# A hybrid encoder step on one core: the later attention's loads, scale rows and gate values in another order

## The chip, the cores and the metric

The kernel runs as one program on one core of a Trainium2 chip. Its time is the device time of one execution in microseconds (us); lower is better. The kernel before took 3911.17 us (median of 3 runs, 3910.19 to 3914.08).

## The reference

One layer of a streaming encoder over two request groups that share the weights: 512 prompt rows and 8 x 16 sample rows, that is 640 rows of 2048 in f32. In the kernel they are five tiles of 128 rows (four prompt tiles, one sample tile).

```
sh1, sc1, g1, sh2, sc2, g2 = split(silu(c) @ w_ada + b_ada)
h = rmsnorm(x, norm1_g) * (1 + sc1) + sh1
za, zg, q, k, v = split(h @ w_in)                   # 2048 -> 5 x 1024
y_conv = silu(layernorm(causal_dwconv(za * sigmoid(zg))))
o = band_attention(q, k, v, bias, 16 heads of 64)
x = x + g1 * (concat(y_conv, o) @ w_out)            # 2048 -> 2048
h2 = rmsnorm(x, norm2_g) * (1 + sc2) + sh2
x = x + g2 * peer(h2)
y = rmsnorm(x, final_g)
```

`peer` makes key queries h2 @ w_pq (2048 -> 2048), scores them against 2 x 128 keys for each of 8 heads, and takes the best 16 of the sums, so each row has 8 x 16 = 128 picks among 16384 experts. For each pick the row of `u_experts` (2048 values) is multiplied with h2 and summed (a dot), gelu of it times the softmax weight is the pick's weight, and the weighted rows of `v_experts` are summed.

## The kernel before

**Two halves.** Tiles 0 and 1 are the first half, tiles 2, 3 and 4 the later half (`TX = 2`, `TY = 3`). The first half goes ahead through attention, output projection, second norm, key queries and key scores. While TensorE (PE) then works on the later half, VectorE (DVE) picks and works off the dots of the first half.

**Dots.** There are 640 steps (`step(n)`, line 2180): 40 groups of 16, one group for each tile and head. A step waits for one gather, in which each of 128 partitions gets one row of `u_experts` (128 x 2048 f32, 1.05 MB), multiplies and sums it (line 2201), and does a piece of the choosing for a coming group. GpSimd (POOL) issues the gathers (line 776) into four buffers: gather n waits for dot n - 4. Steps are laid by hand between DVE's other work, by `steps(k)` calls. Dots 0 to 255 belong to the first half; step 266 begins the build of the first weight matrix.

**The later half on PE.** Query, key and value projection (`quarter_columns`, `quarter_rows`, lines 1119 and 1126), then 16 attention heads, then the output projection: four blocks of 512 columns, each loaded in four quarters of 1 MB, times three tiles, so 12 results (v = 0 to 11 on DVE). DVE adds each to the residual (lines 2292 and 2293) and lays `steps(4)` behind each of the first nine. PE may be six results ahead of it (`o_free`). Behind v = 10 and v = 11 and the last comes `norm_tile` (line 1922), the second norm of tiles 2, 3 and 4. PE turns the tiles over and multiplies them with `w_pq` in four blocks (line 1119); ScalarE (ACT) copies queries and scores out (`keep_queries`, line 1498).

**The entry to attention.** PE makes the first scores of head 0, runs `stay_busy(5, 22)` (22 products of the identity into bank 5, which nothing reads), and then the part of head 0's scores with the cached keys, whose end releases DVE. DVE comes from its 124th dot, clears a buffer, packs the sample queries (line 2265), waits for head 0's bias (line 2241), and reduces the maximum (lines 2252 to 2256). In each head it lays two more dots.

**SyncE's queue (SP).** SP issues nearly all loads of the later half in written order, each behind its own waits: the w_in quarters; the first three value stores (`values_out(0)`); the first w_out block (`load_block(6, ...)`); three more value stores; for each head its bias, and for each pair of heads cached keys and values; behind attention the rows x and g1 (5 MB), then the w_out blocks 7, 8 and 9 with the scale rows (`A2Y`, `n2Y`) and shift rows (`B2Y`) of the second norm between them, then the first block of `w_pq`. Head h's bias waits until the maximum of head h - 2 is done. A quarter waits until PE has used the quarter that it overwrites.

**Behind it.** PE builds a matrix W of pick weights for two tiles (`build`, 64 rounds of one-hot products with DVE and ACT) and multiplies it with all of `v_experts`, 128 pieces of 1 MB (`dense`, line 1328); this twice, for tiles 0 and 1 and for 2 and 3. Tile 4 is done with 128 gathers of `v_experts` rows on DVE (line 2321). `gate_exp(1)` and `gelu(1)` (lines 1590 and 1594) are tile 1's exp of the softmax and gelu of the dots; the latter waits for 256 dots. Step 266 needs both.

Of the kernel before, what the change touches and what calls it, by code (L numbers as in the profile page):

```python
# [5 lines left out]
def hybrid_encoder_step(nc, ins, outs):  # L6
# [56 lines left out]
    with ctx:  # L63
# [312 lines left out]
        def _(sp):  # L376
# [131 lines left out]
            values_out(0)  # L508
            load_block(6, "w_out", 0)
            values_out(1)  # L510
# [16 lines left out]
            for h in range(NH):  # L527
                hp, b = divmod(h, 2)
                if h >= 2:
                    sp.wait_ge(mx_ready, NH + h - 1)  # L530
                sp.dma_start(biasP[:, b], rows(ext_d, [[EXT - 1, P]], 512, h * P * EXT + 127)).then_inc(s_b[b], 16)
                sp.dma_start(biasC[:, b], biasC_d[h]).then_inc(s_b[b], 16)
                if b == 0 and h + 2 < NH:
                    k_cache(hp + 1)
                if b == 1:
                    values(hp)

            def spread(dst, i, s):
# [9 lines left out]
            for b in range(7, 10):  # L548
                load_block(b, "w_out", (b - 6) * PW)
                if b == 7:  # L550
                    spread(A2Y, 1, s_sc2)
                    sp.dma_start(n2Y, n2rows_d[:, :]).then_inc(s_n2, 16)
                if b == 8:
                    sp.wait_ge(s_A2, 3)
                    sp.dma_start(B2Y[0], modrows_d[2, 0]).then_inc(s_sh2, 16)
# [254 lines left out]
        def _(pe):  # L810
# [359 lines left out]
            def scores(h):  # L1170
                hp, b = divmod(h, 2)
                r = slice(DH * b, DH * b + DH)
                q, k = catY[r, CT + hp], kT[r, hp]
                pe.wait_ge(mx_ready, NH + h)
                pe.matmul(PB[0][:, 0:512], q[:, 128:256], k[:, 0:512], start=True, stop=True)
                pe.matmul(PB[1][:, 0:384], q[:, 0:128], k[:, 0:384], start=True, stop=True)
                pe.matmul(PB[2][:, 384:512], q[:, 256:384], k[:, NP:NT], start=True, stop=True)
                if h == 0:
                    stay_busy(5, 22)
                pe.wait_ge(s_qx, hp + 1)  # L1180
                pe.wait_ge(kct_E, hp + 1)
                for s in range(NB):
                    m = pe.matmul(PB[2][:, 256:384], qX[r, s], kCT[r, hp % 2, s], start=(s == 0), stop=(s == NB - 1))  # L1183
                m.then_inc(sc_ready, 1)
# [157 lines left out]
        def _(act):  # L1342
# [155 lines left out]
            def keep_queries(G, dst, tiles):  # L1498
                for n in range(16):
                    act.wait_ge(q_done, 16 * G + n + 1)  # L1500
                    if n >= 2:
# [143 lines left out]

            gate_exp(1)
            gelu(1)
            copy_turned(0)
# [43 lines left out]
        def _(dve):  # L1692
# [539 lines left out]
            for g in range(2):  # L2232
                for k in range(18):
                    choose(g, k)
            steps(124)

# [38 lines left out]
            for h in range(NH):  # L2275
# [6 lines left out]
                steps(1)  # L2282
            steps(16)

# [3 lines left out]
            for v in range(4 * TY):  # L2288
# [4 lines left out]
                TT(x[:, at], x[:, at], wtmp[:, v % 2], ALU.add).then_inc(o_free, 1)  # L2293
                if v == 4:
                    dve.wait_ge(s_sc2, 16 * 2)
                    dve.wait_ge(s_n2, 16)
                    for b in range(2):
                        STT(out=A2Y[b], in0=A2Y[b], scalar=1.0, in1=n2Y, op0=ALU.add, op1=ALU.mult).then_inc(s_A2, 1)
                if v < 3 * TY:
                    steps(4)  # L2300
                elif v == 3 * TY:
                    steps(2)
                    dve.wait_ge(s_A2, 3)
                    dve.wait_ge(s_sh2, 16)
                elif v < 4 * TY:
                    norm_tile(TX + v - 3 * TY - 1, A2Y[0], B2Y[0])
                    steps(1)
            dve.wait_ge(s_sh2, 16 * 2)
# [47 lines left out]
```

## Time and profile before

| What | Value |
|---|---|
| median of 3 runs | 3911.17 us |
| the profiled execution's own time | 3912.98 us |
| its span (first to last instruction) | 3911.2 us |
| PE busy | 3659.4 us, 94% |
| DVE busy | 2665.0 us, 68% |
| ACT / POOL busy | 444.2 / 1022.0 us |
| mean DMA rate, bytes moved | 363 GB/s, 1418.49 MB |
| issuing queues | POOL's gathers q0 848.17 MB; SP's q1 563.29 MB |

All times in the rows are us from the span's start. The span lies 1.8 us under the execution's own time. A row of a timeline has the start, the duration, engine, line and operation, out<-in, and in brackets how long the engine had been idle and what ended that. "SPq" rows are the issuing of transfers, not the transfers. The busy shares are means over the whole span; the change touches some 600 us of it, from 1210 to 1850 us.

### The profile page before, as it was taken

The page shows a single profiled execution, that of the slowest core. Times are in us where ns is not written, and L with a number is a line of the kernel's source. Part 1 is how long each engine was busy: PE and PEld are TensorE (multiplying, and loading weights), DVE is VectorE, ACT ScalarE, POOL GpSimd, SP SyncE. Part 2 cuts the span into 40 slices and gives each one's busy share as a digit, 9 for nine tenths or more (in the row PEclk, how much of TensorE's full clock was granted, in tenths as well). Part 3 has the DMA queues.
Part 4 walks back from the last instruction along what each step waited for, and adds up shares of the span by engine and source line. Part 5 has one row for each costly group of instructions (what it writes and reads, how often), then busy time and mean ns, then how long its engine had stood idle before and what let it go on. Part 6 is the DMA issues. An engine that isn't in the chain of part 4 may idle for free.

```text
span 3911.2 us, 34419 instructions
## 1 busy us (share of the span) xinstructions
PE 3659.4 (94%) x12521; PEld 1929.5 (49%) x12521; DVE 2665.0 (68%) x4253; ACT 444.2 (11%) x975; POOL 1022.0 (26%) x888
## 2 busy tenths in 40 slices
PE   5899999998998898899989999999998899999996
PEld 2566545476543663466734444444465344444443
DVE  1258853157888788878986777767688754555666
ACT  2100004110000440102600000000052000000000
POOL 1000001215324344343232222222233322222331
PEclk8999999998999799999999999999999999999998
DMA  9878773559999899999799999999989999999997
GB/s 387 274 247 275 256 290 128 198 204 405 413 414 417 331 379 413 395 406 361 266 415 421 414 411 422 421 419 418 417 294 358 421 421 380 421 422 422 421 417 310
DMA packets 337760, 1418.49 MB, mean 363 GB/s; under 512 B 26009, under 2 KB 134529, under 8 KB 195742
## 3 DMA queue, kind: packets, MB, share of 16 engines
q0 software_dynamic: 120752, 848.17, 53.8%
q1 hardware_dynamic: 215840, 563.29, 37.8%
q10 hardware_dynamic: 1008, 4.98, 0.3%
q8 instruction: 91, 1.49, 0.2%
q14 instruction: 69, 0.57, 0.0%
HBM read 1390.84 MB, written 47.28 MB: 368 GB/s over the span
## 4 chain that ended last, share of the span: by engine, by line
DMA 50%; PE 31%; issue 12%; DVE 5%; POOL 2%; ACT 1%; DVEq 0%; POOLq 0%; SPq 0%; ACTq 0%
DMA R<-in_u_experts,MS 36%; DMA R<-in_v_experts,MS 10%; PE bank L895 8%; PE bank L926 7%; PE bank L1119 4%; PE bank L1298 3%; DMA R<-in_w_ada 2%; DVE R L2321 2%; PE bank L840 1%; POOL R L776 1%; DVE R L2201 1%; PE bank L1294 1%; PE bank L812 1%; PE bank L1183 1%; DMA R<-in_w_in 1%
## 5 line engine op out<-in xcount | busy, mean ns | idle before, releaser
L776 POOL DMA_INDIRECT R<-in_u_experts,MS x640 | 817.9, 1278 | 1699.1 <-DVE MS L2201 1477.7
L2201 DVE CUSTOM_DVE_ANT_0 R<-R 128x2048 f32<-128x2048 f32 x374 | 856.6, 2291 | 383.3 <-DMA R<-in_u_experts,MS 361.8
L1328 PE MATMUL bank<-R,RB 128*128 128x512 f32 x2304 | 1024.6, 603 | 48.2 <-DMA R<-in_v_experts 48.2
L1328 PE MATMUL bank<-RB 128*128 128x512 f32 x1792 | 778.2, 592 | 0.0
L1328 PEld LDWEIGHTS bank<-R,RB 128*128 128x128 f32 x2304 | 443.1, 193 | 619.6 <-issue 559.1
L2201 DVE CUSTOM_DVE_ANT_0 R<-R,RB 128x2048 f32<-128x2048 f32 x266 | 608.6, 2288 | 124.2 <-DMA R<-in_u_experts,MS 123.4
L1328 PEld LDWEIGHTS bank<-RB 128*128 128x128 f32 x1792 | 340.5, 190 | 428.6 <-issue 428.6
L2321 DVE SCALAR_TENSOR_TENSOR R<-R,MS 128x2048 f32<-128x2048 f32 x128 | 301.5, 2355 | 198.1 <-DMA R<-in_v_experts,MS 197.7
L895 PE MATMUL bank<-RB,R 128*128 128x256 f32 (+1 forms) x1536 | 399.8, 421 | 23.2 <-DMA R<-in_w_pq 18.8
L895 PEld LDWEIGHTS bank<-RB,R 128*128 128x128 f32 x1536 | 294.0, 193 | 122.6 <-DMA R<-in_w_pq 19.3
L1119 PE MATMUL bank<-RB,R 128*128 128x384 f32 x1024 | 334.9, 487 | 10.1 <-DMA R<-in_w_in 8.8
L1126 PE MATMUL bank<-R,RB 128*128 128x512 f32 x576 | 255.7, 606 | 23.5 <-DMA R<-in_w_out 13.9
L926 PE MATMUL bank<-R,RB 128*128 128x512 f32 x640 | 275.8, 592 | 0.5 <-issue 0.5
L1119 PEld LDWEIGHTS bank<-RB,R 128*128 128x128 f32 x1024 | 192.7, 190 | 144.5 <-DMA R<-in_w_in 13.4
L776 POOL DMA_INDIRECT R<-in_v_experts,MS x128 | 135.1, 1056 | 384.2 <-DVE R L2321 359.3
L926 PEld LDWEIGHTS bank<-R,RB 128*128 128x128 f32 x640 | 121.1, 190 | 151.4 <-issue 151.4
L1126 PEld LDWEIGHTS bank<-R,RB 128*128 128x128 f32 x576 | 111.2, 194 | 166.6 <-issue 137.2
L1829 DVE SCALAR_TENSOR_TENSOR RB<-RB,MS 128x512 f32<-128x512 f32 x240 | 175.8, 732 | 0.0
L1298 PE MATMUL bank<-R 128*128 128x128 f32 x1024 | 137.0, 277 | 2.2 <-DVE R L2084 2.2
L1753 DVE TENSOR_TENSOR RB<-bank,RB 9x256 f32<-9x256 f32 x128 | 53.5, 418 | 112.1 <-PE bank L840 108.0
L1298 PEld LDWEIGHTS bank<-R 128*128 128x128 f32 x1024 | 125.9, 194 | 2.8 <-DVE R L2084 2.8
L812 PE MATMUL bank<-MS,RB 128*128 128x128 f32 (+5 forms) x493 | 71.6, 291 | 34.8 <-DMA RB<-in_rel_bias_table 17.5
(355 smaller groups left out, 2248.5 us busy)
## 6 DMA issues: line engine op xcount, KB each, us to landing
R<-in_v_experts SPq DMA_DIRECT2D x144, 1024.0 KB, 9.1
RB<-in_v_experts SPq DMA_DIRECT2D x112, 1024.0 KB, 9.1
R<-in_w_ada SPq DMA_DIRECT2D x48, 2048.0 KB, 14.0
R<-in_w_in SPq DMA_DIRECT2D x20, 2048.0 KB, 18.8
R<-in_w_in SPq DMA_DIRECT2D x24, 1024.0 KB, 33.4
R<-in_w_out SPq DMA_DIRECT2D x8, 2048.0 KB, 8.4
R<-in_w_pq SPq DMA_DIRECT2D x8, 2048.0 KB, 10.6
R<-in_w_out SPq DMA_DIRECT2D x16, 1024.0 KB, 33.0
```

Of the source, the lines that this page charges most:

```text
L776: pool.indirect_dma_start(dst, None, table, bass.IndirectOffsetOnAxis(ap=expert[T_ % 2][:, c:c + 1], axis=0)).then_inc(signal, 16)
L812: return pe.transpose(out, in_, ident[0:k, 0:k])
L895: m = pe.matmul(PB[2 * par + i][:, 0:src.shape[-1]], w, src[:, k], start=(k == 0), stop=(k == KT - 1))
L926: m = pe.matmul(PB[bank][:, :], src[:, 8 * half + i, t * P:(t + 1) * P], wide[:, slot, i, :], start=(half + i == 0), stop=(half + i == 8))
L1119: m = pe.matmul(PB[bank][:, 0:NY], quad[:, q, i, c * P:(c + 1) * P], src[:, 4 * q + i], start=(q + i == 0), stop=(q + i == 6))
L1126: m = pe.matmul(PB[bank][:, :], src[:, 4 * q + i, t * P:(t + 1) * P], quad[:, q, i, :], start=(q + i == 0), stop=(q + i == 6))
L1298: x = pe.matmul(PB[m % 2][:, k * P:(k + 1) * P], oneh[m % 3][:, 1, k], oneh[m % 3][:, 0, k], start=True, stop=True)
L1328: x = pe.matmul(PB[4 * h + q][:, :], W[:, i, h * P:(h + 1) * P], vring[slot][:, q * PW:(q + 1) * PW], start=(i == 0), stop=(i == NKEY - 1))
L1753: t = TT(m, PB[4 + b][32 * g:32 * g + NCND, 0:BW], m, ALU.add)
L1829: ch.mark(STT(out=oP, in0=iP, scalar=w, in1=oP, op0=ALU.mult, op1=ALU.add))
L2201: V.tensor_tensor_reduce(u, u, x, 1.0, 0.0, ALU.mult, ALU.add, dots[t % 2][:, h * TOPK + s:h * TOPK + s + 1]).then_inc(dots_done, 1)
L2321: STT(out=acc, in0=pick_rows[p % NPICK], scalar=weight[TP][:, p:p + 1], in1=acc, op0=ALU.mult, op1=ALU.add).then_inc(v_used, 1)
```

## The change

SP: block 6 of w_out is loaded behind head 3's loads and no longer ahead of the last value stores; the scale rows come behind block 8 and not behind block 7; the first shift rows behind block 9 and not block 8. DVE: 116 dots ahead of attention (124 before), 28 behind it (16), two fewer at v = 9 and one fewer each behind v = 10 and v = 11; the A2 product stands behind v = 7 and not v = 4. Both orders have 212 dots when the last norm tile begins. PE: 34 filler products in head 0 (22), and 2 more ahead of head 1. ACT: tile 1's exp and gelu before the 13th key query of the later half and not behind all 16.

```diff
@@ SP
             values_out(0)
-            load_block(6, "w_out", 0)
             values_out(1)
...
                 if b == 1:
                     values(hp)
+                if h == 3:
+                    load_block(6, "w_out", 0)
...
             for b in range(7, 10):
                 load_block(b, "w_out", (b - 6) * PW)
-                if b == 7:
+                if b == 8:
                     spread(A2Y, 1, s_sc2)
                     sp.dma_start(n2Y, n2rows_d[:, :]).then_inc(s_n2, 16)
-                if b == 8:
+                if b == 9:
                     sp.wait_ge(s_A2, 3)
                     sp.dma_start(B2Y[0], modrows_d[2, 0]).then_inc(s_sh2, 16)
@@ PE, scores(h)
+                if h == 1:
+                    stay_busy(5, 2)
                 pe.wait_ge(mx_ready, NH + h)
...
                 if h == 0:
-                    stay_busy(5, 22)
+                    stay_busy(5, 34)
@@ ACT, keep_queries
                 for n in range(16):
+                    if G and n == 12:
+                        gate_exp(1)
+                        gelu(1)
...
-            gate_exp(1)
-            gelu(1)
             copy_turned(0)
@@ DVE
-            steps(124)
+            steps(116)
...
-            steps(16)
+            steps(28)
...
-                if v == 4:
+                if v == 7:
                     dve.wait_ge(s_sc2, 16 * 2)
...
                 elif v == 3 * TY:
-                    steps(2)
                     dve.wait_ge(s_A2, 3)
                     dve.wait_ge(s_sh2, 16)
                 elif v < 4 * TY:
                     norm_tile(TX + v - 3 * TY - 1, A2Y[0], B2Y[0])
-                    steps(1)
```

SP's queue at the entry to attention, before. `out_new_v` are the value stores, `ext_scratch` and `biasC_scratch` a head's bias, `k_cache` and `v_cache` the cached rows of a pair.

```order
57 L485 DMA R<-in_w_out 128x4x512 x4
58 L496 DMA out_new_v_prompt<-RB 128x512 x2
59 L496 DMA out_new_v_sample<-RB 128x512
60 L531 DMA RB<-ext_scratch 128x512
61 L532 DMA MS<-biasC_scratch 128x128
62 L465 DMA RB<-k_cache_by_pairs 128x1024
```

The same queue now, from the last value stores on; the left-out rows are the loads of heads 0 to 2.

```order
58 L496 DMA out_new_v_sample<-RB 128x512
59 L530 DMA RB<-ext_scratch 128x512
60 L531 DMA MS<-biasC_scratch 128x128
...
72 L520 DMA RB<-out_new_v_prompt 128x4x128
73 L521 DMA RB<-out_new_v_sample 128x128
74 L522 DMA RB<-v_cache_by_pairs 128x1024
75 L485 DMA R<-in_w_out 128x4x512 x4
76 L530 DMA RB<-ext_scratch 128x512
77 L531 DMA MS<-biasC_scratch 128x128
78 L465 DMA RB<-k_cache_by_pairs 128x1024
```

The 4 MB of w_out stood ahead of head 0's bias, and stand now ahead of head 4's.

SP's queue in the output projection, before (`mod_rows` are g1, scale and shift rows, `norm_rows` the norm's gains, `x_scratch` the residual's stores).

```order
125 L541 DMA RB<-mod_rows_scratch 128x2048 x2
126 L485 DMA R<-in_w_out 128x4x512 x4
127 L541 DMA RB<-mod_rows_scratch 128x2048 x2
128 L552 DMA RB<-norm_rows_scratch 128x2048
129 L485 DMA R<-in_w_out 128x4x512 x4
130 L555 DMA RB<-mod_rows_scratch 128x2048
131 L485 DMA R<-in_w_out 128x4x512 x4
132 L560 DMA x_scratch<-RB 128x1536 x3
133 L485 DMA R<-in_w_pq 128x4x512 x4
134 L565 DMA RB<-mod_rows_scratch 128x2048
```

And now:

```order
125 L542 DMA RB<-mod_rows_scratch 128x2048 x2
126 L485 DMA R<-in_w_out 128x4x512 x8
127 L542 DMA RB<-mod_rows_scratch 128x2048 x2
128 L553 DMA RB<-norm_rows_scratch 128x2048
129 L485 DMA R<-in_w_out 128x4x512 x4
130 L556 DMA RB<-mod_rows_scratch 128x2048
131 L561 DMA x_scratch<-RB 128x1536 x3
132 L485 DMA R<-in_w_pq 128x4x512 x4
133 L566 DMA RB<-mod_rows_scratch 128x2048
```

Blocks 7 and 8 follow each other, and the first shift rows stand behind block 9, right ahead of the residual's stores.

ACT at the end of the later key queries, before (L1504 copies a query, L1496 scores, L1590 is the exp, L1594 the gelu):

```order
471 L1504 ACTIVATE MS<-bank 128x384 [waits key_scores,q2_done]
472 L1496 ACTIVATE RB<-bank 128x3x128 [waits key_scores] x2
473 L1590 ACT_TABLE_LOAD
474 L1590 ACTIVATE RB<-RB 128x128 [waits gate_logits]
475 L1594 ACT_TABLE_LOAD
476 L1594 ACTIVATE MS<-MS 128x128 [waits dots]
477 L1608 ACTIVATE MS<-bank 128x128 [waits picks_turned] x2
```

And now (L1510, L1499, L1596 and L1600 are the same four lines):

```order
463 L1510 ACTIVATE MS<-bank 128x384 [waits key_scores,q2_done]
464 L1499 ACTIVATE RB<-bank 128x3x128 [waits key_scores]
465 L1596 ACT_TABLE_LOAD
466 L1596 ACTIVATE RB<-RB 128x128 [waits gate_logits]
467 L1600 ACT_TABLE_LOAD
468 L1600 ACTIVATE MS<-MS 128x128 [waits dots]
469 L1510 ACTIVATE MS<-bank 128x384 [waits key_scores,q2_done]
```

Exp and gelu stand four queries earlier, with their two table loads.

## Rows read from the trace of the kernel before

**Rows 1.** Stretches: busy us of PE, PEld, DVE, ACT, POOL; PE clock, DMA share, GB/s

```profile
1290.00:1300.00 10.00, 6.80 (x22) 5.14 (x22) 7.31 (x19) 3.53 (x9) 3.31 (x2) 0.50 0.36 109
1300.00:1350.00 50.00, 48.73 (x311) 38.24 (x310) 39.75 (x112) 29.24 (x77) 16.83 (x10) 0.83 0.90 318
1350.00:1400.00 50.00, 50.00 (x380) 40.05 (x378) 45.37 (x120) 35.40 (x94) 19.91 (x12) 1.00 1.02 397
1400.00:1440.00 40.00, 35.51 (x245) 27.48 (x245) 37.76 (x83) 23.72 (x62) 24.56 (x12) 0.91 0.90 340
1440.00:1640.00 200.00, 178.44 (x414) 78.97 (x413) 165.69 (x269) 7.75 (x23) 77.77 (x53) 0.95 1.02 415
...
2100.00:2800.00 700.00, 700.00 (x1633) 309.92 (x1632) 499.33 (x826) 4.78 (x6) 175.90 (x174) 1.00 1.01 418
```

**Rows 2.** Timeline of PE from the entry to attention to w_pq

```profile
1244.10 19.15 PE L817 MATMUL bank<-MS 128*128 128x512 f32 x44
1281.76 3.78 PE L1183 MATMUL bank<-RB 64*128 64x128 f32 x16 [18.52 <-DVE RB L2265]
...
1318.79 1.12 PE L1175 MATMUL bank<-RB 64*128 64x512 f32 x2
...
1416.19 1.12 PE L1175 MATMUL bank<-RB 64*128 64x512 f32 x2
...
1438.39 62.07 PE L1126 MATMUL bank<-R,RB 128*128 128x512 f32 x144 [0.63 <-ACT RB L1550]
...
1535.20 84.56 PE L1126 MATMUL bank<-R,RB 128*128 128x512 f32 x192 [12.76 <-DMA R<-in_w_out]
...
1660.85 36.39 PE L1119 MATMUL bank<-RB,R 128*128 128x384 f32 x112 [0.84 <-ACT RB L1490]
```

**Rows 3.** Timeline of DVE, dots and the first head's entry

```profile
1252.54 2.29 DVE L2201 CUSTOM_DVE_ANT_0 R<-R,RB 128x2048 f32<-128x2048 f32 x1 [0.42 <-DMA R<-in_u_experts,MS]
...
1277.78 2.29 DVE L2201 CUSTOM_DVE_ANT_0 R<-R,RB 128x2048 f32<-128x2048 f32 x1 [0.34 <-DMA R<-in_u_experts,MS]
...
1291.19 0.11 DVE L2241 MEMSET RB<- 64x64 f32 x1 [9.49 <-DMA MS<-biasC_scratch]
...
1293.07 2.29 DVE L2201 CUSTOM_DVE_ANT_0 R<-R,RB 128x2048 f32<-128x2048 f32 x1
```

**Rows 4.** Timeline of SP's issues

```profile
1210.74 30.06 SPq L485 DMA_DIRECT2D R<-in_w_out  x4
...
1628.29 5.12 SPq L565 DMA_DIRECT2D RB<-mod_rows_scratch  x1
```

**Rows 5.** Timeline of DVE behind attention, to the last norm

```profile
1434.78 2.29 DVE L2201 CUSTOM_DVE_ANT_0 R<-R,RB 128x2048 f32<-128x2048 f32 x1
1437.59 2.29 DVE L2201 CUSTOM_DVE_ANT_0 R<-R,RB 128x2048 f32<-128x2048 f32 x1
...
1484.07 0.68 DVE L2292 TENSOR_TENSOR MS<-bank,RB 128x512 f32<-128x512 f32 x1
...
1544.24 4.49 DVE L2298 SCALAR_TENSOR_TENSOR RB<-RB 128x2048 f32<-128x2048 f32 x2
...
1619.68 0.68 DVE L2292 TENSOR_TENSOR MS<-bank,RB 128x512 f32<-128x512 f32 x1
...
1649.62 0.16 DVE L1915 TENSOR_REDUCE MS<-MS 128x1 f32<-128x4 f32 x1 [2.24 <-DMA RB<-mod_rows_scratch]
...
1653.65 2.29 DVE L1928 TENSOR_TENSOR RB<-RB 128x2048 f32<-128x2048 f32 x1
```

**Rows 6.** Timeline of ACT and DVE at the start of the first build

```profile
1837.68 1.28 ACT L1590 ACT_TABLE_LOAD   x1
...
1839.39 0.29 DVE L2045 TENSOR_REDUCE MS<-RB 128x8 f32<-128x128 f32 x1 [7.96 <-ACT RB L1590]
...
1848.32 0.60 ACT L1621 ACTIVATE RB<-bank 128x512 f32<-128x512 f32 x1 [4.22 <-DMA R<-RB]
```

**Rows 7.** Timeline of DVE at the end, the last gathered row's sum

```profile
3877.80 2.29 DVE L2121 TENSOR_TENSOR R<-R,RB 128x2048 f32<-128x2048 f32 x1
```

## The prediction

> **What bounds the kernel now.** I read the stretches first, then the timelines of the engines between 1210 and 1850 us, then the end. From 2100 to 2800 us PE is busy 700 of 700 us and the DMA engines stand at 1.01 [rows 1]: the products with `v_experts` and the gathers beside them fill both, and no instruction there changes. The two end together: the last gathered row of `v_experts` is summed at 3877.8 us [rows 7], about when PE ends. So whatever the change does must show as an earlier or later start of w_pq (PE at 1660.85 [rows 2]); from there I carry the shift to the end one to one.
>
> Ahead of w_pq the stretch from 1440 to 1640 us moves 415 GB/s at a share of 1.02 [rows 1]: saturated. The same share with 397 GB/s stands in the middle of attention. Only three stretches leave room: 1290 to 1300 (0.36), 1300 to 1350 (0.90), 1400 to 1440 (0.90). Against 1.02 that is 6.6 + 6.0 + 4.8 = 17.4 us of DMA time. DVE's chain of dots runs along this bound: a gather is 1.05 MB, and dots come 3.16 us apart ahead of attention ((1277.78 - 1252.54) / 8 [rows 3]), 2.81 us apart when no weights load [rows 5]. The last norm starts when its shift rows have landed, at 1649.62, and ends at 1653.65 + 2.29, so near 1655.9 [rows 5]; w_pq starts 5 us behind it.
>
> **Step 1, the entry to attention.** Before, PE's 22 fillers end at 1263.3, it idles 18.52 us for DVE, and then DVE idles 9.49 us for head 0's bias, whose transfer stands behind 4 MB of w_out [rows 2 to 4]. Head 0's maximum is done at 1293.07 [rows 3]. Now the 116th dot ends at 1252.54 + 2.29 = 1254.8 or a little sooner, and ahead of the bias stand only value stores of 0.8 MB; I expect it well ahead of 1265. What is late next is PE itself: 34 fillers take 34 / 22 x 19.15 = 29.6 us and end at 1273.7; the part with the cached keys takes 1.9 at the full clock (3.78 at 0.50), the maximum another 1.9 (1291.19 to 1293.07). That gives 1277.5: 15.6 us earlier. DVE meanwhile idles some 20 us, and the gathers stop when four are in.
>
> The granted clock is 0.50 in 1290 to 1300 and 0.83 in 1300 to 1350, behind PE's 18.52 us of idle [rows 1, 2]. With PE busy until 1275.6 and two more fillers ahead of head 1, I expect 1.00. From head 0's maximum to the scores of head 3 it took 25.7 us; twelve later heads took 8.1 each (1416.19 - 1318.79 [rows 2]), so this could be 16.2. I take 7.5 of the 9.5 us. Together -23.
>
> **Step 2, w_out ahead of head 4's bias.** It is issued at about 1285, behind head 1's maximum. From there to head 4's bias the queue holds 5.7 MB (bias, cached rows and values 1.2, w_out 4.2, the bias 0.3), and DVE asks for six or seven gathers of 1.05 MB beside them: 12.5 MB at 400 GB/s are 31 us, so 1316. DVE needs it at 1308. I take a stall of 7 us (0 to 15). DVE waits, and behind it PE's next scores; head 5's bias has landed by then. Attention ends 16 us earlier than before: 1438.39 becomes 1422.
>
> **Step 3, twelve more dots ahead of the first residual** (28 for 16). Between 2.81 us, DVE's own pace [rows 5], and 3.34, what is left to gathers when PE takes a quarter of w_out (24 of the 144 instructions in 62.07 us [rows 2], 10.4 us) each time: 415 - 101 = 314 GB/s. I take 3.25, near the upper end because DMA is saturated there before: +39 (34 to 40).
>
> **Step 4, first to tenth residual.** Before 1619.68 - 1484.07 = 135.6 us [rows 5]. Now DVE comes later than PE: blocks 6 and 7 end 83 us after 1422, near 1505, and PE waits for residuals, which no longer matters to DVE. PE's wait of 12.76 us for block 8 [rows 2] goes, since scale rows (3 MB) no longer stand ahead of it, but it was not what DVE waited for. DVE's floor is 36 x 2.81 + 9 x 1.3 + 4.5 for A2 = 117.5. By bytes it is 37.7 MB of gathers and about 13 MB (rest of block 8, block 9, scale and shift rows, stores, some w_pq) at 415: 122. Neither is met exactly; I take 124 (117 to 136): -11.6. The tenth residual comes at 1484.1 - 16 + 39 + 124 = 1631, 11.4 us late.
>
> **Step 5, tenth residual to the end of the last norm.** Before 36.2 us, with four dots between. Now none; the first two norms end some 19 us after it. The last shift rows (issued at 1628.29 before [rows 4]) are issued some 3 us after the tenth residual, behind w_pq, which is now issued in one piece after the ninth residual: about 3.6 MB of it, four gathers, 0.8 MB of stores and the rows themselves, 9.6 MB, 23 us. With the norm's 6.3 (1649.62 to 1655.9) that is 29.5 (25.6 to 36.2): -6.7.
>
> **Step 6, exp and gelu.** The 256th dot is done long before the 13th key query arrives, so ACT does not hold PE. At the end 2 x 1.28 us of table loads go from ACT, and DVE's 7.96 us of idle ahead of step 266 is cut short [rows 6]. But the first copy of W waits for the saved scores until 1848.32 [rows 6], and the dot behind step 266's one-hots waits for PE, so it is hidden: 0 (-2 to +1). The Trainium skill (ScalarE: Activation LUTs, What ACT_TABLE_LOAD costs) says that a switch of table costs a drain besides the load, about 2.66 us in all. The trace has 1.28 us, and the next step on ACT begins right behind it. By the page 5.3 us would go from ACT and by the rows 2.6; neither reaches 1848.32.
>
> **Sum.** -23 + 7 + 39 - 11.6 - 6.7 + 0 = +4.7, say +5. On the profiled execution's 3912.98 this is 3918, on the median, which lies 1.8 us lower, 3916. A count of bytes agrees. Both orders have the same 212 dots done at the last norm, so the difference is the DMA time left empty. Before it is 17.4 and some 2.6 in the norms. Now: about 3 ahead of 1250, 15 while DVE waits for PE's fillers, some 4 in and after the stall, 5 at attention's end: 27. That would be +7.
>
> **Rivals.**
> A, faster: w_out falls into attention's empty DMA time and head 4's bias is in time. Then attention ends 23 us earlier, the twelve dots run at DVE's 2.81 (+33.7), the residuals at the floor (-18), the norms -6.7: -14, 3897. For it: 0.90 in 1300 to 1350 and a 12.76 us wait that goes. Against it: 397 GB/s at 1.02 from 1350 on [rows 1], so that the room ends where the load does. 25%.
> B, slower: the gathers take the DMA engines first, and the w_out quarters, in 2 KB pieces, only what they leave. Head 4's bias then comes 15 us late, attention ends 8 us earlier, and with +39 and -3 to -7 in each of steps 4 and 5 the end is at +21, 3932. For it: a bias of 64 KB that kept DVE until 1291.19 behind four quarters issued between 1210.74 and 1240.8 [rows 3, 4]. It decides if the stall at head 4 is over 12 us. 18%. The Trainium skill (DMA: Bandwidth & Descriptors, Queues, rings and completion order) says that a DMA engine takes turns between its rings packet by packet, and that all of SP's transfers share one ring, consumed in order. The trace agrees with the order: the bias behind w_out is the late one.
> C, the filler is the wrong length in the other direction: the bias lands later than 1276 after all, so PE's 12 additional fillers cost nothing and DVE's idle is what the bias makes it. Then step 1 is -8 in place of -15.6, and the total +12, 3923. 12%.
>
> **How the numbers follow.** The forecast (0 to +10 around +5) has 45%. A measurement of this kernel can tell about 0.2%, 7.8 us, from no change. A lies beyond it on the fast side but for its weaker forms, and the forecast has a tail there: faster 0.25. Between: most of the forecast and some of A and C, 0.41. B, most of C and the upper part of the forecast: slower 0.34. The range that leaves out 2 in 10 reaches from A's 3898 to B's 3931; the forecast's own is 3909 to 3923.
>
> **What the changed profile would show.** Step 1: fillers until about 1274 with DVE idle from 1251 to 1276, first head's dot at 1277.5, clock 1.00 up to 1320. Step 2: DVE idle about 7 us in head 4, released by a bias. Steps 3 and 4: first residual near 1507, tenth near 1631, PE waiting for DVE in the output projection, and no wait for block 8. Step 5: last norm's wait ended by shift rows near 1654, w_pq from 1666. Step 6: no table load behind the last key query and DVE still held until the build. It is wrong if w_pq starts ahead of 1653 or behind 1674, or if the end does not move with it: then PE and gathers have slack between 1850 and 3877 that the shares hide.

## The result, and the profile after

The changed kernel took 3940.86 us (median of 4 runs, 3925.53 to 3944.81), the kernel before 3911.62 in the same comparison: ratio 1.0059, 95% interval 1.0036 to 1.0082. A second comparison, with 6 and 23 runs, gave 3944.83 against 3913.92: 1.0082 (1.0056 to 1.0108). The change makes the kernel slower by 0.6 to 0.8%, by the medians 29 and 31 us; 3916 was forecast and the range ended at 3931. (The ratios are those on record; they are not the quotients of the two medians.)

The profiled execution is the fastest of the four, 3925.53 us with a span of 3923.7. PE is busy 3647.2 us (3659.4 before), DVE 2665.8 (2665.0); the same 1418.49 MB move.

The stretches of the kernel after (columns as in [rows 1]):

```profile
1290.00:1300.00 10.00, 0.34 (x4) 0.11 (x1) 0.00 (x0) 0.00 (x0) 0.00 (x0) 0.64 1.03 404
1300.00:1350.00 50.00, 43.68 (x282) 34.14 (x283) 39.66 (x113) 29.35 (x77) 16.45 (x10) 0.83 0.88 317
1350.00:1400.00 50.00, 50.00 (x387) 40.25 (x385) 44.86 (x116) 34.38 (x93) 19.71 (x12) 1.00 1.00 379
1440.00:1640.00 200.00, 156.64 (x351) 67.40 (x349) 169.08 (x267) 4.04 (x11) 85.39 (x56) 0.92 1.01 403
1501.61:1634.05 132.44, 99.08 (x220) 42.84 (x218) 116.13 (x188) 0.00 (x0) 67.60 (x37) 0.90 1.00 398
2100.00:2800.00 700.00, 700.00 (x1633) 309.92 (x1632) 501.00 (x830) 4.78 (x6) 170.84 (x174) 1.00 1.01 419
```

From 1290 to 1300 us PE and DVE do next to nothing while the DMA engines are full: one transfer is waited for. The gap at 1290 is not gone, it has another cause. In 1300 to 1350 clock, share and rate are nearly those of [rows 1] (0.88 and 317 where there were 0.90 and 318).

PE's timeline of the kernel after, against [rows 2]:

```profile
1225.81 29.45 PE L818 MATMUL bank<-MS 128*128 128x512 f32 x68
1306.32 2.07 PE L1178 MATMUL bank<-RB 64*128 64x512 f32 x2 [15.97 <-DVE MS L2260]
1414.33 41.47 PE L1127 MATMUL bank<-R,RB 128*128 128x512 f32 x96 [0.63 <-ACT RB L1556]
1518.65 5.10 PE L1127 MATMUL bank<-R,RB 128*128 128x512 f32 x8 [11.69 <-DVE RB L2297]
1650.13 3.68 PE L813 MATMUL bank<-MS,RB 128*128 128x128 f32 x16 [27.48 <-DVE RB L2297]
1666.00 34.45 PE L1120 MATMUL bank<-RB,R 128*128 128x384 f32 x106 [0.85 <-ACT RB L1493]
```

The first row is the one to look at twice. The fillers start at 1225.81 us, 18.3 us earlier than in [rows 2]. Of what lies ahead of them only the place of block 6 was changed, which SP had issued from 1210.74 on [rows 4]; PE waited less for w_in. Over all 17 profiles of this case the fillers start at 1225.8 to 1248.7 where block 6 is late and at 1231.5 to 1246.9 where it is early, so that the lead is not the work of the change. So starts in this trace can't be set against those of before; distances from the first filler can. To w_pq they are 440.2 us now and 416.75 before, +23.4, where the starts of w_pq themselves differ by 5.15 only.

DVE's timeline of the kernel after, against [rows 3] and [rows 5]: the clearing of a buffer behind the 116th dot, head 0's first dot, the first instruction of heads 3 and 4 (L2245 was L2241), first and tenth residual, the last norm:

```profile
1252.50 0.91 DVE L2277 MEMSET RB<- 128x1024 f32 x1 [0.16 <-issue]
...
1258.96 2.29 DVE L2205 CUSTOM_DVE_ANT_0 R<-R,RB 128x2048 f32<-128x2048 f32 x1
...
1278.82 0.11 DVE L2245 MEMSET RB<- 64x64 f32 x1
...
1304.31 0.11 DVE L2245 MEMSET RB<- 64x64 f32 x1 [17.91 <-DMA MS<-biasC_scratch]
...
1501.61 0.68 DVE L2296 TENSOR_TENSOR MS<-bank,RB 128x512 f32<-128x512 f32 x1
...
1634.05 0.67 DVE L2296 TENSOR_TENSOR MS<-bank,RB 128x512 f32<-128x512 f32 x1
...
1660.24 2.29 DVE L1932 TENSOR_TENSOR RB<-RB 128x2048 f32<-128x2048 f32 x1
```

SP's issues of the kernel after that lead to the wait of 17.91 us: the first of head 3's five small loads, block 6 of w_out, and behind it the two pieces of head 4's bias. The column of durations is how long the queue took over the issuing.

```profile
1266.41 0.32 SPq L530 DMA_DIRECT2D RB<-ext_scratch  x1
...
1270.58 16.48 SPq L485 DMA_DIRECT2D R<-in_w_out  x4
1287.10 7.61 SPq L530 DMA_DIRECT2D RB<-ext_scratch  x1
1294.75 0.53 SPq L531 DMA_DIRECT2D MS<-biasC_scratch  x1
```

Issuing four quarters takes 16.5 us, the first piece of the bias 7.6 more, and DVE is released 9 us after the second was issued. From the issue of block 6 to DVE's release it is 33.7 us. What the two big queues moved from head 3's first load to the start of DVE's wait (1266.41 to 1286.40; packets, MB, share of the DMA engines' time; q0 are the gathers, q1 SP's transfers), and then during the wait (1286.40 to 1304.31):

```profile
q0 software_dynamic: 741, 5.43, 67.3%
q1 hardware_dynamic: 1713, 2.41, 33.1%
...
q1 hardware_dynamic: 2362, 4.20, 63.2%
q0 software_dynamic: 410, 2.95, 40.0%
```

In the kernel before, head 3's first DVE instruction was at 1320.56:

```profile
1320.56 0.11 DVE L2241 MEMSET RB<- 64x64 f32 x1
```

ACT and DVE of the kernel after at the build, against [rows 6], and DVE's end, against [rows 7]:

```profile
1798.02 1.28 ACT L1596 ACT_TABLE_LOAD   x1
1807.10 0.31 ACT L1600 ACTIVATE MS<-MS 128x128 f32<-128x128 f32 x1 [6.17 <-DVE MS L2205]
1846.57 1.89 DVE L2088 SCALAR_TENSOR_TENSOR R<-bank,MS 128x512 f32<-128x512 f32 x3 [6.90 <-PE bank L1288]
1855.61 0.60 ACT L1627 ACTIVATE RB<-bank 128x512 f32<-128x512 f32 x1 [7.28 <-DMA R<-RB]
3890.31 2.29 DVE L2125 TENSOR_TENSOR R<-R,RB 128x2048 f32<-128x2048 f32 x1
```

### The profile page after: what moved, and what is told of

Same layout as the page of the kernel before. It is cut to its first block, busy times and chain, and to the rows that moved or that the text cites. A ratio compares the mean times of both kernels' runs of the same rounds, so it can differ in the third digit from the quotient of the medians.

```text
span 3923.7 us, 34475 instructions
## 1 busy us (share of the span) xinstructions
PE 3647.2 (93%) x12549; PEld 1920.8 (49%) x12549; DVE 2665.8 (68%) x4253; ACT 443.4 (11%) x975; POOL 1058.6 (27%) x888
## 2 busy tenths in 40 slices
DMA packets 337760, 1418.49 MB, mean 362 GB/s; under 512 B 26009, under 2 KB 134529, under 8 KB 195742
## 3 DMA queue, kind: packets, MB, share of 16 engines
q1 hardware_dynamic: 215840, 563.29, 37.7%
## 4 chain that ended last, share of the span: by engine, by line
DMA 47%; PE 35%; issue 10%; DVE 6%; POOL 1%; ACT 1%; DVEq 0%; SPq 0%; POOLq 0%; ACTq 0%
DMA R<-in_u_experts,MS 29%; DMA R<-in_v_experts,MS 10%; PE bank L896 9%; PE bank L1120 7%; PE bank L927 7%; DMA R<-in_w_in 3%; PE bank L1301 3%; DMA R<-in_w_ada 2%; DVE R L2323 2%; PE bank L841 1%; PE bank L1127 1%; DVE R L2205 1%; DMA R<-in_w_pq 1%; POOL R L777 1%; PE bank L1297 1%
## 5 line engine op out<-in xcount | busy, mean ns | idle before, releaser
L777 POOL DMA_INDIRECT R<-in_u_experts,MS x640 | 850.2, 1328 | 1686.1 <-DVE MS L2205 1433.8
L896 PE MATMUL bank<-RB,R 128*128 128x256 f32 (+1 forms) x1536 | 398.7, 420 | 22.7 <-DMA R<-in_w_pq 18.2
## 6 DMA issues: line engine op xcount, KB each, us to landing
R<-in_w_ada SPq DMA_DIRECT2D x48, 2048.0 KB, 14.7
R<-in_w_in SPq DMA_DIRECT2D x20, 2048.0 KB, 18.7
```

Of the source, the lines that this page charges most:

```text
L777: pool.indirect_dma_start(dst, None, table, bass.IndirectOffsetOnAxis(ap=expert[T_ % 2][:, c:c + 1], axis=0)).then_inc(signal, 16)
L896: m = pe.matmul(PB[2 * par + i][:, 0:src.shape[-1]], w, src[:, k], start=(k == 0), stop=(k == KT - 1))
```

## Experiments

All but one were timed in five rounds beside the kernel before on the same chip. "To w_pq" is the distance from PE's first filler to the first product with w_pq in each one's profiled execution; "wait" is DVE's wait for head 4's bias there. Each of these two is read from one execution, and not always from a typical one: the profiled executions of the changed kernel took 3925.5 and 3933.3 us, of "fillers back" 3908.9, of "block 6 and dots back" 3897.0, of "block 6 spread" 3917.9, all 10 to 18 us below their kernel's median.

| Kernel | median us | ratio to before (95%) | to w_pq | wait |
|---|---|---|---|---|
| before / before, profiled again | 3911 to 3917 | | 416.8 / 419.6 | 0 |
| changed / measured again | 3940.9 / 3944.8 | 1.0082 (1.0056 to 1.0108) | 440.2 / 439.7 | 17.9 / 18.2 |
| changed, exp and gelu back | 3947.6 | 1.0081 (1.0054 to 1.0109) | 442.8 | 18.2 |
| changed, scale rows back | 3943.7 | 1.0069 (1.0044 to 1.0093) | 442.7 | 18.9 |
| before + block 6, dots, fillers | 3943.1 | 1.0069 (1.0052 to 1.0086) | 439.0 | 18.1 |
| changed, block 6 back | 3924.5 | 1.0017 (1.0002 to 1.0032) | 416.6 | 1.2 |
| changed, dots back | 3919.7 | 1.0014 (0.9999 to 1.0030) | 414.9 | 16.8 |
| changed, fillers back | 3926.4 | 1.0027 (1.0011 to 1.0043) | 419.4 | 4.5 |
| changed, block 6 behind head 15 | 3928.0 | 1.0027 (1.0013 to 1.0042) | 423.1 | 0 |
| changed, block 6 spread | 3928.2 | 1.0038 (1.0022 to 1.0054) | 429.6 | 10.4 |
| changed, block 6 and dots back | 3914.5 | 0.9998 (0.9984 to 1.0012) | 416.7 | 0 |
| block 6 back, 120/24 dots | 3913.5 | 1.0001 (0.9982 to 1.0020) | 406.9 | 0 |
| block 6 back, 120/20/2/1/1 dots | 3916.3 | 0.9992 (0.9976 to 1.0008) | 417.7 | 0 |
| block 6 spread, dots back | 3912.1 | 0.9982 (0.9968 to 0.9997) | 405.2 | 4.2 |
| block 6 spread, 120/24 dots, 22 fillers | 3918.7 | 1.0007 (0.9996 to 1.0018) | 418.4 | 0 |

**Is the lead of 18 us part of the change?** The changed kernel once more, and the kernel before profiled once more.

> The changed kernel, measured once more against the kernel before. Theory T: the profiled execution shown above began attention some 18 us early by chance (its value projection ended at 1222.1 us, that of the kernel before at 1240.4), and the change itself costs 25 us between there and w_pq: 18 us of stall at head 4 instead of 7, and dots behind attention. Then most runs lie at 3935 to 3945, and in a profile whose value projection ends near 1240 w_pq starts near 1684. Rival L: the lead is made by the change and w_pq is always near 1666; the loss is made behind it, and w_pq starts at 1666 in an execution of 3940 too.

> The kernel before, profiled once more. Both theories: from the first filler to w_pq 417 us (plus or minus 3). From w_pq to the last gathered row's sum the first profile had 2219 us, those of the versions 2225 to 2231. If 2219 comes again, something in the change costs 6 us or more behind w_pq; if it is 2223 or more, that is chance.

PE's timeline of the changed kernel's second profile, with DVE's wait and the last sum's row between:

```profile
1235.12 29.45 PE L818 MATMUL bank<-MS 128*128 128x512 f32 x68
1313.64 0.11 DVE L2245 MEMSET RB<- 64x64 f32 x1 [18.24 <-DMA MS<-biasC_scratch]
1674.80 25.42 PE L1120 MATMUL bank<-RB,R 128*128 128x384 f32 x78 [0.84 <-ACT RB L1493]
3898.08 2.29 DVE L2125 TENSOR_TENSOR R<-R,RB 128x2048 f32<-128x2048 f32 x1
```

The same rows of the kernel before's second profile:

```profile
1231.47 19.15 PE L817 MATMUL bank<-MS 128*128 128x512 f32 x44
1651.03 36.39 PE L1119 MATMUL bank<-RB,R 128*128 128x384 f32 x112 [0.84 <-ACT RB L1490]
3875.40 2.29 DVE L2121 TENSOR_TENSOR R<-R,RB 128x2048 f32<-128x2048 f32 x1
```

Theory T holds by the median and the profile; three of the six runs lie above its 3945. The start of the fillers moves from execution to execution in both kernels (1225.8 and 1235.1; 1244.1 and 1231.5), and the distance to w_pq stays: 440.2 and 439.7; 416.8 and 419.6. In five profiles with the full loss (the two of the changed kernel and the three kernels below it in the table) the execution's own time less the start of its fillers is 2699.7, 2698.2, 2700.4, 2698.7 and 2698.1 us: with the start of the fillers taken off, a spread of 17 us shrinks to 2.3. For the kernel before it is 2668.9 and 2679.1. And from w_pq to the last row's sum (the row shown) the kernel before has 2217.0 us once and 2224.4 the other time, the changed kernel 2224.3 and 2223.3: the 7 us by which its end seemed to fall behind w_pq are chance.

**Exp and gelu.** `gate_exp(1)` and `gelu(1)` behind all queries again.

```diff
-                    if G and n == 12:
-                        gate_exp(1)
-                        gelu(1)
+            gate_exp(1)
+            gelu(1)
             copy_turned(0)
```

> The changed kernel with tile 1's exp and gelu behind all 16 key queries as before. Theory T and rival S: within 4 us of the changed kernel (3936 to 3945). Rival L (the loss is behind w_pq, with ACT's order part of it): 3925 to 3933.

3947.6 against 3944.8 in shared runs: no effect that can be told.

**Scale rows.** The two conditions on SP and the one on DVE are those of before.

```diff
-                if b == 8:
+                if b == 7:
                     spread(A2Y, 1, s_sc2)
...
-                if b == 9:
+                if b == 8:
                     sp.wait_ge(s_A2, 3)
...
-                if v == 7:
+                if v == 4:
```

> The changed kernel with the scale rows behind block 7, the shift rows behind block 8 and the A2 product at v = 4 as before. Theory T: DVE comes later than PE in the output projection, so PE's wait for block 8 comes back (10 us or more) and costs at most 3; w_pq may start 1 to 3 us earlier by the earlier shift rows: 3941 to 3948. Rival W (the row order is what takes 6 to 10 us of the loss): 3932 to 3938.

3943.7. PE waits 16.06 us for block 8 again, and no change in the time can be told: DVE is the later one. Rival W is out.

**Block 6.**

```diff
             values_out(0)
+            load_block(6, "w_out", 0)
             values_out(1)
...
-                if h == 3:
-                    load_block(6, "w_out", 0)
```

> The changed kernel with w_out's block 6 back ahead of the last value stores; all else as changed. Theory T: head 4's stall of 18 us goes, but head 0's bias comes 15 to 19 us later again, so little is won: 3932 to 3943. Rival S (the loss is the stall at head 4 alone): 3918 to 3926.

It took 3924.5: 20 us less, as rival S said. DVE's timeline shows why T's sum for it was wrong:

```profile
1266.80 0.11 DVE L2244 MEMSET RB<- 64x64 f32 x1 [14.55 <-DMA MS<-biasC_scratch]
1306.04 0.11 DVE L2244 MEMSET RB<- 64x64 f32 x1 [1.21 <-DMA MS<-biasC_scratch]
```

Head 0's bias is late again, but the fillers (from 1244.55, 29.45 us long) run beside that wait and end only at 1274.0. It is free. At head 4 there is next to nothing left.

**The dots.**

```diff
-            steps(116)
+            steps(124)
...
-            steps(28)
+            steps(16)
```

with 2, 1 and 1 in the norms as before.

> The changed kernel with the dots laid as before: 124 ahead of attention, 16 behind it, 2 at v = 9 and one behind each of v = 10 and 11. Theory T: 12 dots less behind attention give 39 us, 4 more in and behind the residuals take 12 and some 4 us of waits are lost, the entry comes 5 to 8 us later: 3918 to 3928. Rival S: the dots are only moved and cost the same in either place: 3936 to 3945.

3919.7, as T said, although head 4 still waits:

```profile
1330.00 0.11 DVE L2245 MEMSET RB<- 64x64 f32 x1 [16.80 <-DMA MS<-biasC_scratch]
```

Attention ends 191.0 us behind the first filler, 2.5 later than in the changed kernel, and the first residual comes 48.7 us behind it in place of 87.3. Neither "the stall alone" nor "the dots alone" is the cause: each put back brings w_pq to where it was before (416.6 and 414.9 for 416.8) and takes 20 and 25 us off the median, most of the 31.

**Both back.** Block 6 and the dots as before; fillers, rows, exp and gelu as changed.

> The changed kernel with block 6 back ahead of the last value stores and the dots as before (124, 16, 2, 1, 1): what is left of the change are the fillers (34 and 2), the scale rows behind block 8, and exp and gelu at the 13th query. Theory T: block 6 and the dots each cost 20 to 25 us only where the other is changed too (late block: head 4's stall takes the place of the dots that DVE no longer does; early block: the same for head 0's bias), so both back give not 3900 but about the kernel before with PE's clock kept at 1.00 at the entry, 3903 to 3914. Rival S (each part costs its own 20 to 25 us): 3893 to 3900. Rival R (fillers, rows or gelu cost what the two versions with one part back still lose, 6 to 10 us): 3918 to 3926.

3914.5, at the upper end of T's range. The two do not add up (rival S is out), and the parts left cost nothing (rival R is out). With this run the four combinations are complete. With block 6 early, w_pq comes 416.7 us behind the first filler with 124 dots ahead of attention and 416.6 with 116; with block 6 late it is 414.9 with 124 and 440 with 116. Only the two together cost. The clock fell at the entry all the same, to 0.50 from 1270 to 1290, since DVE with its 124 dots came later than the fillers' end and PE idled 23.56 us: on that T was wrong.

**The fillers.**

```diff
-                if h == 1:
-                    stay_busy(5, 2)
...
-                    stay_busy(5, 34)
+                    stay_busy(5, 22)
```

> The changed kernel with 22 fillers and none ahead of head 1. Theory T: with 116 dots nothing else holds head 0 back, so the scores come about 10 us earlier and DVE's idle at the entry shrinks by that, but head 4's bias is still behind 4 MB of w_out, whose issue moves 10 us earlier with head 1: 3933 to 3938. Rival X (PE's clock falls at the entry and takes all of it back, or the dots' DMA time is what counts): 3942 to 3950.

3926.4, 7 us better than T expected; rival X is out. SP's and DVE's timeline of this kernel:

```profile
1274.43 10.46 SPq L485 DMA_DIRECT2D R<-in_w_out  x4
1302.67 0.11 DVE L2243 MEMSET RB<- 64x64 f32 x1 [4.48 <-DMA MS<-biasC_scratch]
```

The stretch behind its fillers (columns as above):

```profile
1260.00:1280.00 20.00, 16.87 (x57) 12.48 (x56) 14.64 (x40) 9.16 (x23) 7.70 (x4) 0.54 0.64 226
```

The fillers start at 1239.03 here, so block 6 is issued 35.4 us behind them (44.8 in the changed kernel) and head 4's bias is there at 63.6 (78.5). PE's clock is at 0.54 and heads 1 to 3 pass more slowly: from head 1 to head 3 it takes 21.3 us (14.4 in the changed kernel). DVE now wants head 4's bias 26.7 us behind head 3's first load and not 20.0, and the bias is there 31.2 us behind it and not 37.9, with 5.6 MB of gathers in this time and not 8.4. Each takes 6.7 us off the wait. And with all its fillers the changed kernel reaches head 3 later, 53.0 us behind the first filler for 49.6: the fillers put off the first heads, and with them the issue of block 6, and the clock that they kept up gave the time back just where the transfer needed it.

**Are these three the whole?** The kernel before with the late block 6, the 116 and 28 dots and the 34 and 2 fillers; rows, exp and gelu untouched.

> The kernel before with three parts of the change: block 6 behind head 3, the 116 and 28 dots, the 34 and 2 fillers. Scale rows, exp and gelu as before. Theory T: the whole loss, 3940 to 3948. Rival Y (rows and gelu share in it, since each alone could be put back for nothing only while the other stayed): 3928 to 3936.

3943.1, w_pq at 439.0, a wait of 18.1 us: yes, and rival Y is out.

**The wait without its cause.** Block 6 behind head 15, where no bias follows.

```diff
-                if h == 3:
+                if h == 15:
                     load_block(6, "w_out", 0)
```

> The changed kernel with block 6 behind head 15's bias in place of head 3's: no bias stands behind it any more. Theory T: no stall at head 4; w_out's first quarter arrives some 10 us behind attention's end and PE waits for it, but DVE has 28 dots there and hides it: attention ends 18 to 20 us earlier, 3922 to 3930. Rival V (the twelve more dots and w_out then compete behind attention, and what the stall cost is paid there): 3938 to 3946.

3928.0. DVE's row of head 4 and PE's first wait for w_out in this kernel:

```profile
1304.99 0.11 DVE L2245 MEMSET RB<- 64x64 f32 x1
1460.64 9.68 PE L1127 MATMUL bank<-R,RB 128*128 128x512 f32 x17 [6.83 <-DMA R<-in_w_out]
```

Head 4 waits for nothing, attention ends at 167.6 us behind the first filler (188.5), and PE's 6.83 us for w_out lie beside DVE's 28 dots. Of the 20.9 us won at attention's end 17.1 are left at w_pq. This is the cleanest of the comparisons: only the place of one load differs, and the wait goes with 17 us of the time (3928.0 for 3944.8). Rival V is out.

**One quarter of block 6 behind each of heads 3 to 6.**

```diff
-                if h == 3:
-                    load_block(6, "w_out", 0)
+                if 3 <= h < 7:
+                    load_quarter(24 + h - 3, "w_out", 0)
```

> The changed kernel with block 6's four quarters behind heads 3, 4, 5 and 6, one each, in place of all four behind head 3. Theory T: the stall of 18 us at head 4 falls to 5 or less and PE's clock dips no more; the attention ends 12 to 18 us earlier, and the time is 3926 to 3934. Rival V (DMA time is what counts, the stall only shows where it is empty; without it the bias of the heads behind comes late by as much): 3940 to 3946.

3928.2, inside T's range, but not for T's reasons: 1 MB ahead of head 4's bias still makes DVE wait 10.4 us and not 5, the clock still falls, to 0.57 from 1300 to 1320, and attention ends 7 us earlier where T had 12 to 18.

**Looking for a better one.** First 120 dots ahead of attention, with block 6 back, in two forms; then 124 with the spread quarters; last the spread quarters with 22 fillers, none ahead of head 1, and 120 dots ahead and 24 behind.

> The changed kernel with block 6 early, 120 dots ahead of attention and 24 behind it (116 and 28 with block 6 early took 3924). Theory T: DVE idles 14.6 us for head 0's bias and PE's fillers end 38 us behind their start, so four dots ahead cost nothing and four dots less behind attention give 12.9 us: 3908 to 3916. Rival U (the four gathers delay the bias by as much as they are worth): 3920 to 3926.

> Block 6 early, 120 dots ahead of attention, 20 behind it, 2 at v = 9 and one behind each of v = 10 and 11; fillers, rows and gelu as in the changed kernel. The version with 24 behind attention and none at the norms took 3913.5, with w_pq 407 us behind the first filler. Theory T: four dots less behind attention give 12.9 us, in the norms they cost 7 to 8 and in the residuals 3: w_pq 404 to 406 us behind the first filler, 3910 to 3913. Rival N (the norms' empty stretch also delays what follows w_pq by 6 to 8 us, which is why versions without dots there lie above T's sums): 3903 to 3908.

> The dots as before (124, 16, 2, 1, 1), block 6's quarters behind heads 3 to 6, one each, the rest of the change kept. With all four behind head 3 the same kernel took 3919.7. Theory T: the stall at head 4 (16.8 us there) shrinks to some 8 and the attention ends 8 us earlier: 3907 to 3914. Rival V (DMA time that a stall leaves empty is only moved): 3917 to 3923.

> 22 fillers and none ahead of head 1, block 6's quarters behind heads 3 to 6, 120 dots ahead of attention and 24 behind it, scale rows and gelu as in the changed kernel. Theory T: from a_fill (3926.4, stall of 4.5 us at head 4) four dots less behind attention give 12.9 us and the spread quarters up to 4: 3908 to 3914. Rival Z (the stretch from attention to w_pq is full, so that part of what is won ahead of it comes back): 3914 to 3920.

Of these only the spread quarters with the dots as before are faster than the kernel before: 3912.1 against 3916.7 in shared runs, by 0.18% (0.03 to 0.32%). It is the best of a dozen versions and its interval ends close to no change, so that a gain is likely and not shown. T's sum held for it and for the first form with 120 dots; the second form, at 3916.3, lies 3 us above it with w_pq at 417.7 where T had 404 to 406, and rival N, which wanted 3903 to 3908, is out. Its fillers end at 1270.8, 8 us ahead of head 0's bias, and the clock stands at 0.50 from 1280 to 1300; in the first form they end at 1276.3, 2 us ahead of it, and it stays at 1.00. Up to attention's end the two forms are the same code, and yet head 3 comes 65.9 us behind the first filler in the one profile and 52.8 in the other. So this is a difference between two executions and not between two forms, and where the fillers' end and the bias lie this close, the distance from the first filler is not a fixed one. Rival U is out by the first form. The last one, 3918.7, T had put too low; it is in rival Z's range. Its profile has head 3 reached 56.4 us behind the first filler (49.6 with 116 dots) and waits of 4.0, 2.4 and 1.0 us for the bias of heads 6 to 8: probably the four more dots and the quarters compete where the room was; no run separates them. In the spread version with 124 dots too DVE waits for five biases, of heads 4 to 8, 13.8 us in all where one wait of 16.8 was, and attention ends 6.7 us earlier. In two kernels w_pq comes 10 to 14 us nearer to the fillers than in the kernel before and the median falls by 3.6 and 4.6 only. Each distance is that of one execution, and from w_pq to the end the 17 profiles have 2248.6 to 2263.9 us; where the rest goes no run here shows.

## Why the prediction was wrong, step by step

The distances are from PE's first filler, one profile of each kernel; they add up to the +23.4 us at w_pq.

| Step | forecast | measured | from |
|---|---|---|---|
| 1, entry, heads 0 to 3 | -23 | -23.5 | head 3 at 1278.82 - 1225.81 = 53.0; 76.5 |
| 2, block 6 ahead of head 4 | +7 | +17.7 | head 3 to attention's end 135.5; 117.8 |
| 3, twelve dots | +39 | +41.6 | to the first residual 87.3; 45.7 |
| 4, first to tenth residual | -11.6 | -3.2 | 132.4; 135.6 |
| 5, to w_pq | -6.7 | -9.2 | 32.0; 41.2 |
| sum | +5 | +23.4 | |

Of the 18.7 us by which the sum (4.7) was too low, 10.7 are step 2's, 8.4 step 4's and 2.6 step 3's; steps 1 and 5 came 0.5 and 2.5 us better than forecast.

**Step 1 was right**, in its parts too: head 0's maximum was forecast 33.4 us behind the first filler, and the dot behind it starts at 33.2; the bias had landed long before, and the clock was 1.00 from 1250 to 1290. Rival C (bias too late for the fillers) did not come. What the step left out is what a quicker entry does next.

**Step 2 failed; it was mis-sized.** The mechanism was named, the stall was put at 7 us and is 17.9. Its 31 us began with head 3's own loads, behind head 1's maximum. They are issued when forecast (40.6 us behind the first filler for 40.9), but the bias lets DVE go 37.9 us later, at 1304.31 (37.8 to 38.6 in the other four profiles with the full loss). The rate was right, 397 GB/s for 400; the bytes were not. Until the release 15.0 MB pass where I had 12.5: 8.4 MB of gathers for 6.8, which fits DVE's quicker heads (with the fillers back it is 5.6), and 6.6 MB of SP's for 5.7, the rest being small loads issued just ahead of these and behind them. That is 6.6 us. The other 3.3 us lie at the other end: heads 1 to 3 follow each other in 7.2 us, where I still counted with the pace of later heads, and DVE wants the bias 60.6 us behind the first filler and not 63.9. With both, the forecast's 8 (taken as 7) becomes 17.9. The full clock that step 1 took as a gain of 7.5 us was, in step 2, time less for the transfer; the forecast booked the gain and not its price. Putting the fillers back shows this (the bias is wanted 6.7 us later and the wait is 4.5), and moving the load shows what the stall is worth (17 us).

**Step 3 was near** (+41.6 for +39), and it is what makes the stall count. Fewer dots ahead of attention are a loan: they bring attention's end forward and are paid for behind it. Where nothing holds up head 4 they bring 21 to 28 us (attention ends at 167 to 170 with 116 dots, at 191 to 196 with 124, at 184 where the quarters are spread), and steps 3 to 5 then ask for 29. With the stall they bring 6 against the kernel before and 2.5 against the changed kernel with its dots back.

**Step 4 gave 8 us less.** By [rows 1] I took 415 GB/s; the stretch from the first to the tenth residual had 398, at a share of 1.00. 132.4 us at 398 are 52.7 MB, by the trace 38.0 of gathers and 14.7 of others where I had 37.7 and 13. At 415 the same bytes take 127 us: about 5 us are the rate, the rest bytes. Why the rate is lower is not shown; the same stretch before moved 17.9 MB of others at 415. Steps 3 and 4 are better read as one: 27.4 forecast, 38.4 measured, and 37.7 with the scale rows back, where they split into 47.4 and -9.7.

**Step 5 was near, step 6 right.** The last norm was to wait for its shift rows until 1654; it begins at 1656.22 and no wait for shift rows is left in the norms (the only one over 2 us is 3.10 for the residual's stores). Exp and gelu are out of the way at 1807, the copy of W waits for the saved scores as forecast (7.28 us), and moving them back does nothing.

**The carry to the end** was the place where the forecast could be told wrong by its own words, and the first profile seemed to do so: w_pq at 1666.00, forecast to the microsecond, and the end 12.5 us late. Both were chance. The forecast of 1666 came true by a lead of 18 us and a loss of 23, and the second profile of the kernel before has the missing 7 us behind w_pq as well.

**The rivals.** B, with 18%, had the outcome: it decides if the stall at head 4 is over 12 us, attention ends 8 us earlier (5.8), and the end is +21; at w_pq it was +23.4. Its reason, the gathers first on the DMA engines and w_out only on what they leave, came in part. From head 3's first load to DVE's wait the gathers had 67% of the engines' time and SP's transfers 33%; during the wait it was 40% and 63%. So SP's loads got the smaller part as long as DVE asked for gathers, but they were not held back until the gathers were through. B also said nothing of the sooner need, so that its price came out by luck in part. The medians lie 29 and 31 us apart, the profiles' own times from the first filler on 25 (2699 against the mean of 2669 and 2679); what the remaining 4 to 6 us are is open. A fell: w_out did not fit into attention's empty DMA time. The range, which ended at B's own value, had no room for B coming a little worse than priced.

## What to carry to other kernels

Where a large load is put into a queue, compare two times from the same point: how long it and what stands behind it take, and how soon the first of those is needed; everything that speeds up the work between them (a clock kept high, less work ahead) comes off the second, and what it asks of the same DMA engines lengthens the first. Put the load where nothing urgent follows (17 us here), or cut it into pieces (the wait at head 4 went from 18 to 10.4 us). And measure from a mark inside the trace that lies ahead of the change: two executions of one kernel differed by 9 to 13 us at such a mark here, about half of what was looked for. Such a distance can still move where two events lie close together, as it did by 13 us between two profiles of the same code up to attention's end.

## What the runs showed of the hardware that was not expected

- Issuing 4 MB in four transfers kept SP's queue for 16.5 to 18.6 us in the five profiles with the full loss, and the small transfer behind it for 7.6 to 7.7 more; in the kernel with 22 fillers, where fewer gathers ran beside it, for 10.5 and 3.1. With one 1 MB quarter ahead the issue took 0.45 us, and the bias was still waited for 10.4 us.
- A TensorE near half clock was no loss where a transfer set the pace: with 14 filler products fewer and 0.54 granted from 1260 to 1280 the kernel was 18 us faster than with them and 1.00 in the first four heads.
- A DMA share of 1.00 to 1.02 stood for 379 to 419 GB/s: 379 in the middle of attention, 398 to 415 in the output projection, 419 in the stretch from 2100 to 2800 us. A share says that the engines are full, not what they carry.
